# Working off 32 experts one routing group in turn instead of one group after the other

## The reference

```python
g_logits = xt @ w_gr + b_gr                      # 4 groups
g_idx = argmax(g_logits); g_prob = softmax(g_logits)[g_idx]
e_logits = (xt @ w_er + b_er).reshape(t, 4, 8)[g_idx]   # 8 experts of that group
top_v, top_i = top_k(e_logits, 2)
wts = g_prob * softmax(top_v)
eid = g_idx * 8 + top_i                          # expert numbers 0 to 31
h = silu(xb @ w_gate[e]) * (xb @ w_up[e])        # xb: the tokens of expert e; 1024 -> 512
y += wt * (h @ w_down[e])                        # 512 -> 1024
```

## Time and profile before

| | us |
|---|---|
| median of 3 runs | 1616.34 (1616.0 to 1616.87) |
| the profiled execution, its own time | 1616.23 |
| its span, first to last instruction | 1614.1 |
| TensorE busy | 1447.2 (90%) |
| VectorE busy | 705.7 (44%) |
| ScalarE busy | 488.8 (30%) |
| mean DMA rate over the span | 209 GB/s |
| the experts' stage | about 284 to 808 |

### The profile page before, as it was taken

The page is one execution under the profiler, slowest core; times in us unless marked ns, Lnnn a source line. Parts: engine busy times, 40 slices in busy tenths (PEclk is TensorE's granted clock), DMA queues, the critical chain, the costliest instruction groups (busy, mean ns, idle before and its releaser), DMA issues.

```text
span 1614.1 us, 18013 instructions
## 1 busy us (share of the span) xinstructions
PE 1447.2 (90%) x6858; PEld 1006.7 (62%) x6858; DVE 705.7 (44%) x1297; ACT 488.8 (30%) x723; POOL 38.6 (2%) x73
## 2 busy tenths in 40 slices
PE   6999997999898988898818999998999999999986
PEld 5786776444443433343216888776888888888765
DVE  4567737211011021010054756455256666666635
ACT  6462532110010100010043222324244445444532
POOL 2010000000000000000020110000000000000000
PEclk9999997999999999999959999998999999999988
DMA  8737335699999964999873553121212121121101
GB/s 355 310 131 263 139 119 209 276 426 426 427 426 427 427 268 163 391 423 429 351 296 131 196 208 131 65 80 53 105 53 105 53 85 73 52 105 52 53 1 65
DMA packets 36811, 336.88 MB, mean 209 GB/s; under 512 B 4560, under 2 KB 4688, under 8 KB 18384
## 3 DMA queue, kind: packets, MB, share of 16 engines
q1 hardware_dynamic: 29632, 304.69, 47.0%
q0 software_dynamic: 6624, 29.89, 5.2%
q10 hardware_dynamic: 432, 0.60, 0.1%
HBM read 312.62 MB, written 22.54 MB: 208 GB/s over the span
## 4 chain that ended last, share of the span: by engine, by line
PE 51%; DVE 2%; issue 2%; ACT 2%; DMA 2%; POOL 0%; DVEq 0%; SPq 0%; ACTq 0%; POOLq 0%
PE ps L290 50%; DMA spare<-in_wts_dram 1%; PE ps L718 1%; ACT ar L860 1%; DVE b_NL L1293 0%; PE ps L296 0%; DMA ar<-y_scratch,rt 0%; DVE ar L1285 0%; ACT b_NH L869 0%; DVE ar L1959 0%; DVE ar L1244 0%; DVE hres L1769 0%; DMA y_scratch<-gate 0%; POOL ar L2035 0%; ACT ar L1214 0%
## 5 line engine op out<-in xcount | busy, mean ns | idle before, releaser
L290 PE MATMUL ps<-ring,ar 128*64 128x512 f32 x800 | 244.3, 610 | 15.8 <-issue 10.7
L290 PE MATMUL ps<-ar 128*64 128x512 f32 (+5 forms) x798 | 231.4, 482 | 18.3 <-DVE ar L1589 6.8
L290 PE MATMUL ps<-b_NH,b_WH 128*128 128x512 f32 x704 | 185.6, 399 | 11.0 <-ACT b_NH L869 5.9
L290 PE MATMUL ps<-b_NH,b_WL 128*128 128x512 f32 x704 | 180.2, 391 | 0.0
L1226 DVE TENSOR_TENSOR b_WL<-ring,b_WH 128x1024 fp32r<-128x1024 f32 x112 | 136.6, 1220 | 94.5 <-ACT b_WH L812 94.5
L290 PE MATMUL ps<-b_NL,b_WH 128*128 128x512 f32 x704 | 174.4, 390 | 0.0
L812 ACT ACTIVATE b_WH<-ring 128x1024 fp32r<-128x1024 f32 x112 | 118.3, 1057 | 161.7 <-PE ps L290 159.9
L290 PEld LDWEIGHTS ps<-ar 128*64 128x64 f32 (+3 forms) x798 | 97.5, 163 | 100.5 <-issue 93.1
L290 PEld LDWEIGHTS ps<-b_NH,b_WH 128*128 128x128 f32 x704 | 129.7, 189 | 39.5 <-ACT b_NH L869 11.7
L290 PEld LDWEIGHTS ps<-ring,ar 128*64 128x64 f32 x800 | 77.8, 140 | 118.6 <-issue 117.0
L290 PEld LDWEIGHTS ps<-b_NH,b_WL 128*128 128x128 f32 x704 | 133.0, 189 | 27.9
(11 more groups left out here) (269 smaller groups left out, 1879.5 us busy)
## 6 DMA issues: line engine op xcount, KB each, us to landing
ring<-in_wts_dram SPq DMA_DIRECT2D x84, 2048.0 KB, 13.6
ar<-in_wts_dram SPq DMA_DIRECT2D x24, 2048.0 KB, 19.4
spare<-in_wts_dram SPq DMA_DIRECT2D x24, 2048.0 KB, 19.0
ring<-in_wmod_dram SPq DMA_DIRECT2D x24, 512.0 KB, 4.9
ar<-in_wmod_dram POOLq DMA_DIRECT2D x24, 512.0 KB, 4.1
y_scratch<-gate POOLq DMA_DIRECT2D x11, 1024.0 KB, 21.3
y_scratch<-gate SPq DMA_DIRECT2D x44, 128.0 KB, 15.7
y_scratch<-ar SPq DMA_DIRECT2D x24, 128.0 KB, 15.9
```

Of the source, the lines that this page charges most:

```text
L290: return pe.matmul(o, l, m, start=start, stop=stop, skip_group_check=True)
```

## The change

The panels are laid out, and with them the experts processed, in the order 0, 8, 16, 24, 1, 9, ...; the router's expert columns and their bias are permuted in the same way on the host. Position n now holds expert `8 * (n % 4) + n // 4`. On the chip one instruction changes: the sum that masks the other groups adds the four group values along the innermost axis instead of spreading each over eight neighbours.

```diff
-            signals(dve.tensor_tensor(EM.rearrange("p t (g e) -> p (t g) e", g=4),
-                                      EL.rearrange("p t (g e) -> p (t g) e", g=4),
-                                      bc(last(ogt.rearrange("p t g -> p (t g)")), 128, 16, 8), ALU.add))
+            signals(dve.tensor_tensor(EM.rearrange("p t (e g) -> p t e g", g=4), EL.rearrange("p t (e g) -> p t e g", g=4),
+                                      bc(ogt.rearrange("p t (o g) -> p t o g", o=1), 128, 4, 8, 4), ALU.add))
+EXPERTS = [8 * (n % 4) + n // 4 for n in range(NE)]
...
-    for e in range(NE):
+    for e in EXPERTS:
...
-        np.pad(np.concatenate([w["b_group_router"][0], w["b_expert_router"][0]]), (0, 92)).reshape(128, 1),
+        np.pad(np.concatenate([w["b_group_router"][0], w["b_expert_router"][0][EXPERTS]]), (0, 92)).reshape(128, 1),
...
-         "wr": np.pad(np.concatenate([feat(w["w_group_router"][0]), feat(w["w_expert_router"][0])], axis=2),
+         "wr": np.pad(np.concatenate([feat(w["w_group_router"][0]), feat(w["w_expert_router"][0][:, EXPERTS])], axis=2),
```

## The result

The changed kernel is slower: a median of 1621.88 us (1617.49 to 1626.65, 17 runs) against 1615.80 (1610.56 to 1622.22, 17 runs) of the kernel before on the same chips. The ratio is 1.0043, with a 95% interval of 1.0028 to 1.0057. The forecast was 1616.6 and no difference that can be measured. The value lies just inside the range, whose upper end (1622) had been put there for rival 2; the direction was missed. The profiled execution took 1623.70 us, 7.5 above that of before.

A forecast was written before the change was run, and what follows sets the result against it. Memory sets the experts' stage: bytes / rate plus DMA idle time. Idle 12.1 + 2.2 + 20.2 + 2.2 = 36.7 against 37.5 (-0.8), plus 1.1, gives +0.3 us on 1616.34: 1616.6, range 1611.5 to 1622.

The forecast's parts named there:

- rival 2: TensorE's clock falls inside a second block: 3.4 us each, 1620.0 for one block, 1623.4 for both; chance 0.18.
- part 1: Order of experts: the two second blocks move from positions 19 and 20 to 14 and 18; counts of work stay.
- part 3: Behind each block: ScalarE's wait for stores, now paid twice; 2.2 us idle each, 1.1 more lost for the second.
- part 5: Rest: VectorE's changed mask sum costs 0 (bounds -0.26 and +0.1 us); `places` and `weigh` keep their positions.
- parts 2 and 4: Blocks at 14 and 18: each 28.63 us from `up` to first result; DMA holes 12.1 and 20.2 us idle.
- rival 1: First block's stores land without holding ScalarE: 6.6 and 3.3 us less than 1616.6, giving 1606.7; chance 0.11.

The follow-up runs named there:

- e10: Changed kernel's layout and mask sum, experts exchanged inside the third group so the blocks stand at positions 18 and 22; 1619.91 us, 1.0022 to the kernel before.
- e3: Kernel before, old layout and mask sum, experts exchanged inside the third group so the blocks stand at positions 18 and 22; 1618.32 us, ratio 1.0028.
- e13: Changed kernel plus six matmuls of no use in TensorE's wait at each block's start; 1616.53 us, 1.0013 to the kernel before.
- e5: The changed kernel once more, unaltered, for a second profile; 1620.69 us, 1.0033 to the kernel before.
- e1: Changed kernel without ScalarE's else-branch wait for the stores of earlier second blocks; 1606.02 us, 0.9944 to the kernel before.

## Why the prediction was wrong

**Where the blocks go (part 1), that each has a wait behind it (part 3), and what the mask sum costs (part 5)** were right: positions 14 and 18, two waits of line 1016 on line 1048, a mask sum of 264 ns, e10 and e3 within each other's intervals.

**The step that failed is the length of the blocks in parts 2 and 4**: "597.64 - 569.01 = 28.63 us". The kernel before had two blocks, 28.63 and 30.32 us. I put the 1.7 us of the second down to `places` standing before its one-hots and took the first for both. The row against it stood in the rows: the block at position 20 began with four matmuls in 1.86 us behind a wait of 3.31 us. The block at 19 had the same wait, and VectorE was done with `places` and `weigh` (line 1642) well before the block and then idle itself, as the trace of before shows:

```profile
572.29 1.08 PE L290 MATMUL ps<-xhi,ar 128*64 128x512 f32 x4 [3.31 <-DVE ar L1710]
```
```profile
603.46 1.14 DVE L1642 TENSOR_SCALAR ar<-picks,sm 128x256 f32<-128x256 f32 x4
608.39 0.42 DVE L1654 TENSOR_TENSOR ar<-ar,ps 128x256 f32<-128x256 f32 x1 [3.79 <-ACT ar L1003]
```

So VectorE was not late at 20; the clock was low. In the new order both blocks pay it, 30.3 and 31.4 to 31.6. As no panel was issued during a block, each us of it is a us of DMA hole: 1.7 + 3.0 = 4.7 us in the first profile, which with the forecast's 1616.6 makes 1621.3. e13 gives the blocks their 28.5 us, and the kernel is at 1.0013 with 38.1 us idle (forecast 36.7). That was rival 2, with a price somewhat too high (3.4 us a block, 1623.4 for both) and a chance of 0.18, mostly because one stretch with a clock of 1.00 was held against it. One row of a two-valued quantity was read as its value. What makes the clock fall in one block and not in another stays open: in the new layout it fell in 10 of 10, in the old in 2 of 6.

The clock in the blocks isn't the whole of what spacing costs. In e3, with both blocks at 28.6 us, the kernel is still 2 to 7 us slower than before (1.0014 to 1.0043); there the second wait is paid as in the new order, and the first hole is 15.0 us idle and not 12.1.

**Smaller, beside that step**: the holes behind the blocks were 2.7 and 3.9 us idle for 2.2 each in the first profile (1.9 and 1.8 in e5). In that first profile the clock was at half for 10.3 and 13.7 us around these waits.

**The price of the wait in rival 1** was too low: 9.9 us for both, measured 14 to 16 (e1). That e1's 1606.0 us lies at the 1606.7 of rival 1 is luck: rival 1 started from 1616.6, some 4 to 5 us too low, with blocks of 28.6 us where e1 has 30.3. In the sum only the second wait counts as new, at 2.2 + 1.1 us, so this price hid how much of the change the wait decides.

**The Trainium skill's rule** on the clock ("TensorE: Matmul & The Clock Gate", section "HAM oscillation — how this bites in real kernels") says that a wait for DMA lets the clock fall and the work behind it start slow. It was weighed as speaking against this change. The traces agree in direction, though the wait here was for VectorE: behind 3.3 us of it groups of four matmuls took 1.76 to 1.98 us for 1.04 to 1.08. They don't agree everywhere: in e3 the same wait left the clock at full rate, at both blocks.

## What to carry to other kernels

Where memory sets the pace, as in this stage, moving long pieces of compute apart helped only by the stock of loads that the queue regained between them, and a wait that stopped the issuing of loads could cost more than that; look for such waits first. Here a wait in an else branch, there to keep a count in order, cost 14 to 16 us for two, while the order of experts gave some 3 to 5 us once it was gone. Where a duration appears twice in a trace with two values, price both before taking the smaller.

## What had not been expected of the hardware

Behind a wait of 3.3 us between two dense pieces of TensorE work the clock fell in 12 of 16 second blocks, and in both of the changed kernel in both of its profiles. So the same step had two prices, 28.6 and 30.1 to 31.6 us, and a new order of work can bring the dearer one; position alone doesn't decide, as 18 and 22 were cheap in e3 and dear in e10. Six matmuls without use in that wait kept the clock up in four blocks of four and seem to pay for themselves: 1.0013 against 1.0033 to 1.0043, with intervals that overlap. A store of 128 KB issued behind three loads of 2 MB was waited for some 17 us (641.55 to 659.20); the three loads ahead of it are 14.8 us of that by an estimate from their bytes and 426 GB/s.
